# A 64x64 block inverse inside a linear-attention recurrence: from four array quarters at once to lane after lane on two

## The reference

```python
def _rwkv7_step(state, inp):
    r_t, w_t, k_t, v_t, a_t, b_t = inp
    sa = jnp.einsum('bhij,bhj->bhi', state, a_t)
    state = (state * w_t[:, :, None, :]
             + sa[..., None] * b_t[:, :, None, :]
             + v_t[..., None] * k_t[:, :, None, :])
    y = jnp.einsum('bhij,bhj->bhi', state, r_t)
    return state, y
```

## Time and profile before

| | |
|---|---|
| median of 3 runs | 2487.11 us |
| span of the profiled execution | 2481.7 us (the page gives no other time for it) |
| TensorE busy | 2444.9 us, 99% |
| VectorE busy | 1410.0 us, 57% |
| ScalarE busy | 1074.4 us, 43% |
| the recurrence | from about 294 us to about 520 us of the span |
| inner products (L775) | 1280 records |
| outer products (L785) | 1280 records |

### The profile page before, as it was taken

How to read it: one execution, slowest core, us unless ns; L and a number is a source line. 1 busy time by engine, 2 the same in 40 slices (tenths; PEclk the granted TensorE clock), 3 DMA queues, 4 the chain that set the end, 5 groups by cost and what they waited for, 6 DMA issues and landing times.

```text
span 2481.7 us, 39434 instructions
## 1 busy us (share of the span) xinstructions
PE 2444.9 (99%) x15550; PEld 2003.2 (81%) x15550; DVE 1410.0 (57%) x1743; ACT 1074.4 (43%) x1347; POOL 126.0 (5%) x166
## 2 busy tenths in 40 slices
PE   8999999999999999999999999999999999999997
PEld 5888788877888888888887788888788888888886
DVE  6688566676744454454446544666745445454445
ACT  4454355444444444443334344453544444443332
POOL 1000235420000000000000000000000000000000
PEclk9999999999999999999999999999999999999999
DMA  7556411255666666665665565445566666666564
GB/s 233 179 195 205 136 42 38 66 208 188 196 192 188 186 193 186 188 188 193 193 195 198 195 193 188 143 167 190 170 187 192 188 186 193 186 194 221 189 194 143
DMA packets 225435, 440.87 MB, mean 178 GB/s; under 512 B 13472, under 2 KB 23744, under 8 KB 224224
## 3 DMA queue, kind: packets, MB, share of 16 engines
q1 hardware_dynamic: 221760, 417.38, 54.1%
q0 software_dynamic: 3552, 21.73, 2.6%
HBM read 436.96 MB, written 2.10 MB: 177 GB/s over the span
## 4 chain that ended last, share of the span: by engine, by line
PE 94%; DVE 3%; ACT 1%; issue 1%; DMA 1%; POOL 0%; DVEq 0%; ACTq 0%; SPq 0%; POOLq 0%
PE ps L595 25%; PE ps L597 25%; PE ps L596 25%; PE ps L892 3%; PE ps L1075 1%; PE ps L775 1%; PE ps L785 1%; PE ps L1103 1%; PE ps L622 1%; PE ps L624 1%; PE ps L623 1%; PE ps L882 1%; PE ps L836 1%; DVE wlo L1684 1%; PE ps L740 1%
## 5 line engine op out<-in xcount | busy, mean ns | idle before, releaser
L1246 ACT CAST whi<-raw 128x1024 fp32r<-128x1024 f32 x735 | 772.5, 1052 | 1145.9 <-PE ps L597 1080.1
L1684 DVE TENSOR_TENSOR wlo<-raw,whi 128x1024 fp32r<-128x1024 f32 x549 | 670.1, 1225 | 622.2 <-ACT whi L1246 620.3
L595 PE MATMUL ps<-whi,ahi 128*128 128x512 f32 x2172 | 851.5, 392 | 2.8 <-DVE wlo L1684 2.8
L597 PE MATMUL ps<-whi,alo 128*128 128x512 f32 x2172 | 845.6, 389 | 0.0
L596 PE MATMUL ps<-wlo,ahi 128*128 128x512 f32 x2172 | 845.1, 389 | 0.0
L595 PEld LDWEIGHTS ps<-whi,ahi 128*128 128x128 f32 x2172 | 407.8, 188 | 87.6 <-DVE wlo L1684 3.6
L597 PEld LDWEIGHTS ps<-whi,alo 128*128 128x128 f32 x2172 | 407.7, 188 | 85.5
L596 PEld LDWEIGHTS ps<-wlo,ahi 128*128 128x128 f32 x2172 | 407.9, 188 | 84.4 <-issue 1.0
L2015 DVE TENSOR_TENSOR wlo<-raw,whi 128x1024 fp32r<-128x1024 f32 x193 | 236.2, 1225 | 249.4 <-ACT whi L1246 247.4
L595 PE MATMUL ps<-whi,hThi 128*128 128x512 f32 x656 | 255.4, 389 | 0.0
L597 PE MATMUL ps<-whi,hTlo 128*128 128x512 f32 x656 | 255.2, 389 | 0.0
(11 more groups left out here) (317 smaller groups left out, 1933.8 us busy)
## 6 DMA issues: line engine op xcount, KB each, us to landing
raw<-w_up SPq DMA_DIRECT2D x176, 512.0 KB, 3.6
raw<-w_down SPq DMA_DIRECT2D x176, 512.0 KB, 4.0
raw<-w_gate SPq DMA_DIRECT2D x170, 512.0 KB, 3.6
raw<-w_k SPq DMA_DIRECT2D x32, 512.0 KB, 3.8
raw<-w_r SPq DMA_DIRECT2D x32, 512.0 KB, 4.4
raw<-w_v SPq DMA_DIRECT2D x32, 512.0 KB, 3.7
raw<-w_o SPq DMA_DIRECT2D x32, 512.0 KB, 4.8
raw<-kv_v SPq DMA_DIRECT2D x32, 512.0 KB, 3.7
```

The source lines that it names most:

```text
L595: mm(o, hi[:, k, tok], whi[:, s, k2, :], start=(k == 0), stop=False)
L597: last = mm(o, lo[:, k, tok], whi[:, s, k2, :], start=False, stop=(k == kt - 1))
L1246: nc.scalar.copy(whi[:, s], src).then_inc(hi_done, 1)
L1684: V.tensor_tensor(wlo[:, s], src, whi[:, s].bitcast(F32), ALU.subtract).then_inc(split_done, 1)
```

## The change

Both lanes now use the straight quarters: lane 0 and lane 1 have the same `half(u)` for input and output. In `inner` and `outer` on TensorE lane 1's eight matmuls come first and lane 0's eight after them, each half with its own wait and its own signal (`x_set`, `inv_made`, `z_set`, `xt_made`, `xt_set` of each lane instead of one for both). VectorE masks each lane with an instruction of its own and turns each lane when that lane is there. XS is gone, with ScalarE's two half copies; ScalarE copies lane 1's XT like lane 0's, after VectorE has turned lane 1. In level 1 ScalarE's other work for group s - 1 (`aside`) comes behind both copies and no longer between them. The first block is turned lane by lane too, and `first` is gone.

```diff
-            def quarters(place):
+            def lane(place):
                 for j in range(4):
-                    for a in range(2):
-                        for u in range(2):
-                            last = place(j, j // TT, j % TT, a, half(u), half(u ^ a))
+                    for u in range(2):
+                        last = place(j, j // TT, j % TT, u)
                 return last
 
             def inner(g, l):
-                if l == 1 and g:
-                    pe.wait_ge(ixt_set, 5 * g)
-                pe.wait_ge(ix_set, 5 * g + l)
-                quarters(lambda j, h, t, a, u, v: mm(ps[v, a, half(j)], G[g % 2][u, a, 0, t, 0, h], X[u, a, half(j)],
-                                                     start=True, stop=True)).then_inc(iz_made, 1)
+                for a in (1, 0):
+                    q = lq[a]
+                    if l == 1 and g and not a:
+                        pe.wait_ge(q["xt_set"], 5 * g)
+                    pe.wait_ge(q["x_set"], 5 * g + l)
+                    lane(lambda j, h, t, u: mm(ps[half(u), a, half(j)], G[g % 2][half(u), a, 0, t, 0, h], X[half(u), a, half(j)],
+                                               start=True, stop=True)).then_inc(q["inv_made"], 1)
 
             def outer(g, l):
-                if l == 1:
-                    pe.wait_ge(moved, g + 1)
-                else:
-                    pe.wait_ge(ixt_set, 5 * g + l - 1)
-                pe.wait_ge(iz_set, 5 * g + l)
-                quarters(lambda j, h, t, a, u, v: mm(ps[u, 2 * a, (1 - a) * T + j * CHUNK:(1 - a) * T + (j + 1) * CHUNK], Z[v, a, half(j)],
-                                                     XS[v, half(j)] if a else XT[g % 2][v, 0, half(j)],
-                                                     start=True, stop=True)).then_inc(ixt_made, 1)
+                for a in (1, 0):
+                    q = lq[a]
+                    if g or l > 1:
+                        pe.wait_ge(q["xt_set"], 5 * g + l - 1)
+                    pe.wait_ge(q["z_set"], 5 * g + l)
+                    lane(lambda j, h, t, u: mm(ps[half(u), 2 * a, (1 - a) * T + j * CHUNK:(1 - a) * T + (j + 1) * CHUNK], Z[half(u), a, half(j)],
+                                               XT[g % 2][half(u), a, half(j)], start=True, stop=True)).then_inc(q["xt_made"], 1)
...
 # ScalarE
             def outer(g, l, aside=None):
-                act.wait_ge(ixt_made, 5 * g + l)
+                act.wait_ge(lq[0]["xt_made"], 5 * g + l)
+                nc.scalar.copy(XT[g % 2][:, 0], ps[:, 0, T:2 * T]).then_inc(lq[0]["xt_set"], 1)
+                act.wait_ge(lq[1]["xt_made"], 5 * g + l)
                 if l < 5:
-                    nc.scalar.copy(XT[g % 2][:, 0], ps[:, 0, T:2 * T]).then_inc(xt_kept, 1)
-                    if aside:
-                        aside()
-                    act.wait_ge(ix_turned, 4 * g + l)
-                    move(XS, ps[:, 2, 0:T]).then_inc(ixt_set, 1)
-                else:
-                    nc.scalar.copy(XT[g % 2][:, 0], ps[:, 0, T:2 * T])
-                    nc.scalar.copy(XT[g % 2][:, 1], ps[:, 2, 0:T]).then_inc(ixt_set, 1)
+                    act.wait_ge(lq[1]["x_set"], 5 * g + l + 1)
+                nc.scalar.copy(XT[g % 2][:, 1], ps[:, 2, 0:T]).then_inc(lq[1]["xt_set"], 1)
+                if aside:
+                    aside()
...
 # VectorE
             def inner(g, l):
-                dve.wait_ge(iz_made, 5 * g + l)
-                V.tensor_tensor(Z.rearrange("p l (j c) -> p l j c", c=CHUNK), ps[:, 0:2, 0:4 * CHUNK].rearrange("p l (j c) -> p l j c", c=CHUNK),
-                                mask_lv[:, l].unsqueeze(1).unsqueeze(1).broadcast_to([P, 2, 4, CHUNK]), ALU.mult).then_inc(iz_set, 1)
+                for a in (1, 0):
+                    q = lq[a]
+                    dve.wait_ge(q["inv_made"], 5 * g + l)
+                    V.tensor_tensor(Z[:, a].rearrange("p (j c) -> p j c", c=CHUNK), ps[:, a, 0:4 * CHUNK].rearrange("p (j c) -> p j c", c=CHUNK),
+                                    mask_lv[:, l].unsqueeze(1).broadcast_to([P, 4, CHUNK]), ALU.mult).then_inc(q["z_set"], 1)
 
             def outer(g, l):
-                dve.wait_ge(ixt_made, 5 * g + l)
-                V.transpose(X[:, 1], ps[:, 2, 0:T]).then_inc(ix_turned, 1)
-                dve.wait_ge(xt_kept, 4 * g + l)
-                V.transpose(X[:, 0], ps[:, 0, T:2 * T]).then_inc(ix_set, 1)
+                for a in (1, 0):
+                    q = lq[a]
+                    dve.wait_ge(q["xt_made" if a else "xt_set"], 5 * g + l)
+                    V.transpose(X[:, a], ps[:, 2 * a, (1 - a) * T:(2 - a) * T]).then_inc(q["x_set"], 1)
```

More of the change, by code:

```diff
@@ L250, in trunk @@
         XT = [tmp(place, 2, 4 * CHUNK) for place in ("rec2", "a2t")]
-        X, Z, XS = tmp("rec2", 2, 4 * CHUNK), tmp("rec2", 2, 4 * CHUNK), tmp("rec2", 4 * CHUNK)
+        X, Z = tmp("rec2", 2, 4 * CHUNK), tmp("rec2", 2, 4 * CHUNK)
         BK = tmp("rec2", 2, 2, TT, P)
@@ L304, in trunk @@
         cum_made, cum_read, decay_done, nat_done = (sem(n) for n in ("cum_made", "cum_read", "decay_done", "nat_done"))
-        ix_set, iz_made, iz_set, ixt_made, ixt_set, first_set, moved = (
-            sem(n) for n in ("ix_set", "iz_made", "iz_set", "ixt_made", "ixt_set", "first_set", "moved"))
         y_centred, y_squared = sem("y_centred"), sem("y_squared")
         names = ("tr_made arT_set bkT_set g_made g_set av_made av_set uhw_made uhw_set "
-                 "post_made s_made s_set y_made y_set")
+                 "post_made s_made s_set y_made y_set "
+                 "first_set x_set inv_made z_set xt_made xt_set")
         lq = [{n: sem(f"lane{s}_{n}") for n in names.split()} for s in range(2)]
@@ L317, in trunk @@
         fill_used, fill_copied = sem("fill_used"), sem("fill_copied")
-        ix_turned, xt_kept = sem("ix_turned"), sem("xt_kept")
         nk_done = sem("nk_done")
@@ L789, in solutions @@
             def solutions(g):
-                pe.wait_ge(ixt_set, 5 * (g + 1))
                 for q in lq:
+                    pe.wait_ge(q["xt_set"], 5 * (g + 1))
                     pe.wait_ge(q["av_set"], min(g + 2, GROUPS))
@@ L1380, in keep @@
                 nc.scalar.copy(V_[:, :, g * 2 * P:(g + 1) * 2 * P], ps[:, 3, :].rearrange("p (t c) -> p t c", t=TT)).then_inc(fill_copied, 1)
-            def first(g):
-                act.wait_ge(first_set, g + 1)
-                move(XS, XT[g % 2][:, 1]).then_inc(moved, 1)
             def squares(g):
@@ L1420, in _ @@
                 value_part(0, a)
-            first(0)
             decays(1)
@@ L1458, in _ @@
                 outer(s, 5)
-                if more:
-                    first(s + 1)
                 if s in (2, 6):
@@ L1834, in first_block @@
                 dve.wait_ge(q["g_set"], g + 1)
[L1835 to L1841, removed]
@@ L1843, in inner @@
-            def inner(g, l):
-                dve.wait_ge(iz_made, 5 * g + l)
-                V.tensor_tensor(Z.rearrange("p l (j c) -> p l j c", c=CHUNK), ps[:, 0:2, 0:4 * CHUNK].rearrange("p l (j c) -> p l j c", c=CHUNK),
-                                mask_lv[:, l].unsqueeze(1).unsqueeze(1).broadcast_to([P, 2, 4, CHUNK]), ALU.mult).then_inc(iz_set, 1)
+                V.tensor_tensor(XT[g % 2][:, a].rearrange("p (h t c) -> p h t c", h=2, t=TT),
+                                G[g % 2][:, a, 0, :, 0].rearrange("p t h c -> p h t c"),
+                                mask_lv[:, 0].unsqueeze(1).unsqueeze(1).broadcast_to([P, 2, TT, CHUNK]), ALU.mult).then_inc(q["first_set"], 1)
@@ new lines, in first_block @@
+                dve.wait_ge(q["first_set"], g + 1)
+                V.transpose(X[:, a], XT[g % 2][:, a]).then_inc(q["x_set"], 1)
+            def inner(g, l):
+                for a in (1, 0):
[3 more added lines that the diff above has]
+                                    mask_lv[:, l].unsqueeze(1).broadcast_to([P, 4, CHUNK]), ALU.mult).then_inc(q["z_set"], 1)
```

## The result

The changed kernel takes 2518.07 us (median of 4 runs, 2516.41 to 2521.21) against 2486.87 us before (4 runs, 2484.1 to 2488.41). The ratio is 1.0127 with a 95% interval of 1.0113 to 1.0142: 31.2 us slower, 28 to 35 by the interval. The spans of the two profiled executions lie 2516.4 - 2481.7 = 34.7 us apart; that is more than 31.2 because the profiled execution of before was the fastest of its four (2484.1, 2.8 us under the median) and that of the changed kernel lay 0.8 us over its median. Forecast were 34.6 us and 2521.7 us.

What follows compares the result with a forecast made beforehand. The prediction took TensorE's nearly gapless queue in the recurrence to bound the kernel: 37.6 us for longer products, minus 3.5 for closed holes, plus 0.5 for waits, made 34.6 us more, 2521.7 us; range 2512 to 2530.

Steps and rivals of the forecast that it cites:

- The queue: Recurrence stage: a queue of TensorE work with almost no holes, its length the sum of what is queued; 4.3 us idle.
- The main term: Inner and outer products: 16 rounds for 8 on two quarters, 0.47 us more each, 37.6 us over 80 products.
- What comes back: TensorE's holes in the recurrence mostly close, such as L785 behind L794: 3.5 us back, of 4.3 at most.
- (B): Partly hidden, 10%: records of crossed quarters slide one or two rounds into the lanes' products, 4.7 to 9.3 us less, 2512 to 2517.
- VectorE and ScalarE: Recurrence: split masks cost VectorE at most 6 us, hidden; ScalarE's saved copies gain nothing; tighter aside and lane waits, 0.5 us.
- the aside: Level 1, ScalarE's work now behind both copies: ends 0.37 us later, stays hidden by 0.1 us; 0.7 us if it misses.
- (C): Hand-over between lanes in each product costs a restart of 0.15 us, 12 us more over 80 products: 2534 us; 8%.
- (D): A lane's two quarters collide writing one bank and take turns, 32 rounds a product: 112 us more, about 2599 us; 2%.
- (E): Not slower, 3%: levels wait for VectorE, so an earlier mask saves 0.27 us in each of 40 levels, 10.8 us: 2476 us.

Runs made afterwards that it cites:

- Two masks: The kernel before with only VectorE's 128x512 mask cut into two of 128x256, lane 1's first, one signal behind the second: 2486.38 us, ratio 0.9998.

## Why the prediction was right

**The queue.** That the stage is a sum of TensorE's work held. Half the rounds of the changed kernel give back 34.7 us, twice the matmuls add at least the rounds, and the mask as two instructions costs nothing.

**The main term.** 80 products at 0.47 us was read from L845 beside L775. The product grew by 0.46 us in a plain place. The straight quarters alone cost 29.1 us, in a kernel with no other part of the change but the missing XS and its copies, and this is the experiment that shows the cause. The 48 plain steps give 21.9 / 48 = 0.456 us each, 36.5 us for 80 products: 1.1 us less than the 37.6. The rest is what came back.

**What comes back.** The size was near. The 31 other steps grew by 10.8 us, where 31 x 0.456 = 14.1 would be full price, so 3.3 us came back in the traces, against 3.5 - 0.5 = 3.0 in the sum. By the medians 37.6 - 31.2 = 6.4 us are missing: 1.1 and 3.3 as above, and some 2 us that lie within the spread of the runs.

The place was right for a part only. The hole at L785 behind L794, which is a wait for the mask, did go: the step from inner to outer product of level 1 in slot 3 grew from 1.60 to 1.86 us, 0.26 for 0.47. The prediction missed a second hole right behind it. Before, L806 waited for ScalarE's copy of lane 1's solutions (L1397 writes what `lane1_uhw_set` stands for) and started 0.05 us behind its end; from the last L785 record, at 373.64, it is 0.17 us where a round is 0.058:

```profile
373.17 0.59 ACT L1397 COPY a2t<-ps 128x512 f32<-128x512 f32 x1 [0.30 <-PE ps L794]
...
373.81 0.36 PE L806 MATMUL ps<-rec,a2t 64*64 64x64 f32 x8
```

In the changed kernel the copy (L1388) ends at 385.16 + 0.58 = 385.74 us, just before the longer product is through, and the step from outer to inner product grew from 1.75 to 2.05 us, 0.30 for 0.47:

```profile
385.16 0.58 ACT L1388 COPY a2t<-ps 128x512 f32<-128x512 f32 x1 [0.81 <-PE ps L792]
```

The start times are the same within 0.01 us up to L806 in slots 1 to 5, so the two holes make about 0.37 us in each, close to 2 of the 3.3 us. Whether the other 1.3 us are stalls that lie elsewhere now or matmuls that slide ahead, as in rival (B), the traces don't settle. The windows show none of this, 4.15 us idle for 4.30: a record's own time is 0.218 us and a round 0.058, so a wait of 0.16 us behind a small matmul leaves no gap in the busy time. The 4.3 us were therefore no upper bound for what waiting less could save. Stalls for issue, which the prediction left as they were, are 3.6 us for 2.8; "Two masks" had 4.4 with TensorE's list unchanged, so that this difference says nothing.

**VectorE and ScalarE.** The new mask is 422 ns against the 0.42 us taken, the transposes are unchanged, and the aside came as near as said: it ends at 387.35 + 0.58 = 387.93 us and L804 starts at 387.99.

```profile
387.35 0.58 ACT L1352 COPY a2t<-ps 64x512 f32<-64x512 f32 x1
...
387.99 0.36 PE L804 MATMUL ps<-rec,a2t 64*64 64x64 f32 x8
```

**Rivals.** (B), a slide of crossed quarters into the lane's rounds, is there, but shortens nothing at the solutions:

```profile
383.09 1.09 PE L774 MATMUL ps<-rec,a2t 64*64 64x64 f32 x30
383.97 0.33 PE L792 MATMUL ps<-big,rec 64*64 64x128 f32 x2
384.01 0.23 PE L774 MATMUL ps<-rec,a2t 64*64 64x64 f32 x2
384.07 1.04 PE L792 MATMUL ps<-big,rec 64*64 64x128 f32 x30
384.95 1.04 PE L784 MATMUL ps<-a2t,rec 64*64 64x64 f32 x30
385.81 0.27 PE L804 MATMUL ps<-rec,a2t 64*64 64x64 f32 x1
```

Two records of L792 start ahead of the last two of L774, but the other 30 start 384.07 - 383.09 = 0.98 us behind it, which is the 0.51 us of before and the full 0.47; L792, which needs the straight quarters too, then takes its 0.88 us. By the prediction's own sign for (B), a slot that grows by under 3.7 us, it fits one slot of seven, and 2518.07 us lies above its range.

(C), a restart at each hand-over, fell: 32 records take 1.15 us with the hand-over and 1.15 us without it. The 26 ns for an increment, by the Trainium skill's "TensorE: Matmul & The Clock Gate", section "The cost: per-tile semaphore tail", isn't seen in this pace either, with one more increment in a product; it may be in a tail that lies under the next piece, which no run shows. (D), two quarters taking turns at one bank, fell as well: the changed product puts both halves into one bank and has the pace of two records in 0.058 us. (E) fell: two masks on the four quarters save nothing. The lane by lane order saves a little where TensorE does wait for the mask: L784 starts 0.98 us behind L792 in the changed kernel, and 1.15 us in the kernel with the straight quarters alone, which masks both lanes at once.

What stays open is what exactly makes the stalls put down to issue. They grow with the density of small matmuls (none on TensorE's matmuls with half of them in a product, 19.4 us with twice as many), and with twice as many half of the instruction pieces come 3.3 to 4 us apart, near the least distance that any trace has. That fits a limit in the supply of instructions, but it isn't shown: no run changed the supply alone.

## What to carry to other kernels

Before splitting small matmuls into independent streams, count the rounds on the fullest quarter of the array: four 64x64 matmuls on four quarters cost as much as two on two, so a regrouping that drops the crossed quarters doubles the product, however early its halves are ready. Latency is worth buying only where TensorE waits; a page on which VectorE and ScalarE wait for TensorE says that nearly the full price is paid, here 31 of 37 us. And the order within the queue counts as much as the placing, since TensorE reached only about three rounds ahead for an idle quarter here.

## What the runs showed of the hardware

The reach-ahead has a size: with each lane's eight matmuls in a row on separate quarters, 0.97 us a product stand between 0.69 (fully side by side) and 1.15 (one lane after the other), three rounds of eight regained. A round's price goes with the columns that run through it: L794's 32 records of 64x128, eight rounds on four quarters, take 0.88 us, 0.11 us a round, where the 64x64 products have 0.058.

Many small matmuls have a cost beside their rounds: with 64 records in a product TensorE's matmuls waited 19.4 us for issue over the stage, with 30 of 62 instruction pieces 3.3 to 4 us behind the one before, though each undisturbed product kept its pace of four records in 0.058 us. That the pieces are the cause is an inference.
